# Two siblings' edits in one 24,000-instruction block kernel: opening loads, router zeroing and first gather, score banks, out-projection banks

## The reference, cut to what matters

```python
def first_block(x, ...):
    h = _layer_norm(x, ln_in_g, ln_in_b)
    mix = _token_mixer(h, ...)            # h @ w_in, gated delta rule over 8 heads, spatial gating, w_o
    h = _layer_norm(ALPHA * h + mix, ln1_g, ln1_b)
    ffn = _hier_moe(h, ...)               # top 2 of 32 experts for each token
    return _layer_norm(ALPHA * h + ffn, ln2_g, ln2_b)

def _hier_moe(x, ...):
    pg = softmax(x @ w_rg + b_rg); grp = argmax(pg)
    top_v, top_i = top_k((x @ w_re + b_re) of that group, 2)
    ...                                   # rows sorted by expert
    y = (silu(x_pad @ w1[e]) * (x_pad @ w3[e])) @ w2[e]

def second_block(x, meta_tokens, ...):
    h = concat(meta, x)                   # 16 + 512 rows
    q, k, v, xr, gr, g_merge = split(rmsnorm(h) @ w_in)
    attn = gqa(rope(rmsnorm(q)), rope(rmsnorm(k)), v)        # 8 heads, softmax(q k) v
    rnn = rg_lru(conv(xr), ..., lam) * gelu(gr)              # uses 8 * log_sigmoid(lam)
    h = h + (sigmoid(g_a) * attn + sigmoid(g_r) * rnn) @ w_out
    return (h + (silu(g) * u) @ w_ffn_out)[16:]              # g, u of rmsnorm(h) @ w_ffn_in
```

## Time and profile before

| | us |
|---|---|
| median of 3 runs | 2288.48 (2287.21 to 2293.3) |
| the profiled execution, its own time | 2291.81 |
| span in its profile | 2290.0 |
| TensorE busy | 2064.2 (90%) |
| VectorE, ScalarE, GpSimd busy | 950.8, 644.4, 454.5 |
| mean granted TensorE clock | 0.946 of full speed |

### The profile page before, as it was taken

The page is one execution under the profiler, slowest core; times in us unless marked ns, Lnnn a source line. Parts: engine busy times, 40 slices in busy tenths (PEclk is TensorE's granted clock), DMA queues, the critical chain, the costliest instruction groups (busy, mean ns, idle before and its releaser), DMA issues.

```text
span 2290.0 us, 24322 instructions
## 1 busy us (share of the span) xinstructions
PE 2064.2 (90%) x10160; PEld 1515.5 (66%) x10160; DVE 950.8 (42%) x1370; ACT 644.4 (28%) x969; POOL 454.5 (20%) x311
## 2 busy tenths in 40 slices
PE   5999999999999969888788879898898888999999
PEld 4879888888887753333333337676665666888787
DVE  6864444433323661111011125864554883222333
ACT  3442332321323201000000024343135754222221
POOL 4432132232332511111111011320002310000021
PEclk8899999999999979999899989999999998999999
DMA  4662231221324367999999964302111033322220
GB/s 156 202 184 61 56 88 42 38 74 38 74 37 150 138 246 306 407 410 410 403 412 412 417 280 173 108 2 82 46 47 46 37 111 110 110 94 90 84 82 37
DMA packets 97513, 360.75 MB, mean 158 GB/s; under 512 B 9834, under 2 KB 34572, under 8 KB 85112
## 3 DMA queue, kind: packets, MB, share of 16 engines
q1 hardware_dynamic: 84752, 332.76, 40.4%
q0 software_dynamic: 8240, 19.00, 2.5%
q10 hardware_dynamic: 4408, 7.40, 1.0%
HBM read 338.41 MB, written 29.10 MB: 160 GB/s over the span
## 4 chain that ended last, share of the span: by engine, by line
PE 79%; DVE 9%; ACT 5%; issue 5%; POOL 1%; DMA 1%; ACTq 0%; SPq 0%; DVEq 0%; POOLq 0%
PE ps L269 75%; PE ps L273 4%; ACT ST L265 1%; DVE H L259 1%; ACT L265 1%; DVE ST L253 1%; DVE BG L253 1%; ACT M L265 1%; DVE WL L253 0%; POOL WL L253 0%; DVE ST L2829 0%; DMA BG<-h1d,toki 0%; DVE BG L259 0%; DVE ML L253 0%; ACT M L266 0%
## 5 line engine op out<-in xcount | busy, mean ns | idle before, releaser
L269 PE MATMUL ps<-W,BG 128*64 128x512 f32 x672 | 202.1, 643 | 31.5 <-issue 31.4
L269 PE MATMUL ps<-XH,WS 128*128 128x512 f32 x704 | 218.6, 392 | 0.0
L269 PE MATMUL ps<-HTH,WL 128*128 128x512 f32 x448 | 182.4, 407 | 0.0
L269 PEld LDWEIGHTS ps<-ST 128*128 128x128 f32 x1376 | 168.4, 193 | 8.7 <-POOL ST L253 1.7
L269 PE MATMUL ps<-ST 128*128 128x64 f32 (+1 forms) x1376 | 168.7, 274 | 1.2 <-POOL ST L253 1.0
L269 PEld LDWEIGHTS ps<-XH,WS 128*128 128x128 f32 x704 | 133.5, 190 | 28.0
L269 PE MATMUL ps<-M,BG 128*64 128x512 f32 (+1 forms) x336 | 122.1, 550 | 31.2 <-DVE H L259 13.7
L2100 DVE COPY BG<-ps 128x512 f32<-128x512 f32 x32 | 22.1, 692 | 302.0 <-PE ps L269 302.0
L269 PE MATMUL ps<-XL,WS 128*128 128x512 f32 x352 | 138.3, 393 | 5.0 <-DVE XL L253 5.0
L269 PEld LDWEIGHTS ps<-W,BG 128*64 128x64 f32 x672 | 61.6, 147 | 120.8 <-issue 119.5
L263 ACT ACTIVATE BG<-ps 128x512 f32<-128x512 f32 x48 | 28.5, 595 | 381.3 <-PE ps L273 350.0
(11 more groups left out here) (384 smaller groups left out, 4392.9 us busy)
## 6 DMA issues: line engine op xcount, KB each, us to landing
W<-in_w SPq DMA_DIRECT2D x42, 2048.0 KB, 26.6
W<-in_w_in SPq DMA_DIRECT2D x27, 2048.0 KB, 10.4
ST<-in_w SPq DMA_DIRECT2D x14, 2048.0 KB, 25.6
U<-in_w SPq DMA_DIRECT2D x14, 2048.0 KB, 27.2
M<-in_w SPq DMA_DIRECT2D x13, 2048.0 KB
HT<-in_w SPq DMA_DIRECT2D x13, 2048.0 KB, 27.6
W<-in_w_ffn_in SPq DMA_DIRECT2D x22, 1024.0 KB, 7.7
ypad<-BG SPq DMA_DIRECT2D x23, 512.0 KB, 15.0
```

Source lines behind the costliest of these rows:

```text
L269: return p.e.matmul(o, lhsT=l, rhs=r, start=start, stop=stop, skip_group_check=True)
```

## The change

It joins edits of two siblings.
- *Opening.* The loads that ScalarE issued (small projection's weights and rows, layer norm rows, level masks) move to SyncE's list, behind the first weight load; the level masks come last, behind the second weight load. Jobs T0 and T1 are split ahead of d0, and d1 is split after T5. GpSimd subtracts d0's low part first and converts the level masks only in step 4 of `g_qk`; the meaning of counts 1 and 2 of `first_done` is exchanged accordingly.
- *Router and experts.* The zeroing of the gathered rows' buffers moves from GpSimd to ScalarE (a copy times zero). `s_expert_x(0)` stands ahead of the four loads for later stages, and the load of slot 6 (the seventh weights) also waits for the first gather.
- *Recurrence constants.* `v_lambda` and `s_lambda` move from the head of the middle stage into step 4 of the expert loop.
- *Attention.* `f.wide` holds the bank pair of the last `x` tile. Scores skip that pair if another is free, and if it is the next in the list, the transposes of the step before come first.
- *Out-projection.* Tile (m, y) lies in bank 2m + 1 - y; the steps of the norm behind it are reordered, and `s_turn3` is cut in halves.

The diff, with context lines and repeated renumberings of semaphore counts left out:

```diff
@@ -464,12 +464,19 @@
                     q.e.dma_start(cst[:, :], cst_d[:, 0:C_LV]).then_inc(c_cst, 16)
-            for n in range(2):
-                q_weight(n)
+            q_weight(0)
+            q.e.dma_start(wab_raw, w_in[:, 6144:6272].rearrange("(k p) n -> p k n", p=P)).then_inc(c_ab, 16)
+            q.e.dma_start(abr[:, 0:16], b_in[6144:6160].partition_broadcast(P)).then_inc(c_ab, 16)
+            q.e.dma_start(abr[:, 16:24], a["dn_dt_bias"][0].partition_broadcast(P)).then_inc(c_ab, 16)
+            q.e.dma_start(abr[:, 24:32], a["dn_a_log"][0].partition_broadcast(P)).then_inc(c_ab, 16)
+            for r, x in enumerate((a["ln_in_g"], a["ln_in_b"])):
+                q.e.dma_start(rows_in0[:, r, :], x.partition_broadcast(P)).then_inc(c_row[r], 16)
+            q_weight(1)
+            q.e.dma_start(lvf, cst_d[:, C_LV:C_N]).then_inc(c_lv, 16)
...
-            q.wait_ge(first_done, 2)
+            q.wait_ge(first_done, 1)
             for b in range(part, NZ, 3):
@@ -495,11 +502,6 @@
                 s_ln(0, i)
-            for r, x in enumerate((a["ln_in_g"], a["ln_in_b"])):
-                s.e.dma_start(rows_in0[:, r, :], x.partition_broadcast(P)).then_inc(c_row[r], 16)
-            s.e.dma_start(lvf, cst_d[:, C_LV:C_N]).then_inc(c_lv, 16)
-            s_ab_load()
-            s_split_w(0)
             s.wait_ge(*B["pc"].free())
@@ -508,16 +510,15 @@
                 s_split(("T", k))
-            s_split_w(1)
+                if k in (1, 5):
+                    s_split_w(k // 4)
...
             g.e.memset(z_t, 0.0).then_inc(g.up())
-            g.wait_ge(c_lv, 16)
-            g.e.tensor_copy(lv[:, :], lvf).then_inc(first_done)
+            low_split_w(g, 0)
             g.wait_ge(*g.now)
             g.e.memset(xpz, 0.0).then_inc(first_done)
-            low_split_w(g, 0)
             low_split_w(g, 1)
@@ -571,7 +572,7 @@
-        JOBS = [("d", 0)] + [("T", k) for k in range(8)] + [("d", 1), ("d", 2), "ab"] + [("d", n) for n in range(3, 24)]
+        JOBS = [("T", 0), ("T", 1), ("d", 0)] + [("T", k) for k in range(2, 6)] + [("d", 1), ("T", 6), ("T", 7), ("d", 2), "ab"] + [("d", n) for n in range(3, 24)]
         JOBS += [("v", 0, i) for i in range(4)] + [("v", 1, i) for i in range(4)]
@@ -684,7 +685,7 @@
             if n < 3:
-                s.wait_ge(first_done, 2)
+                s.wait_ge(first_done, 1)
             else:
@@ -936,6 +931,9 @@
                     low_split(g, "ab")
+                if n == 4:
+                    g.wait_ge(c_lv, 16)
+                    g.e.tensor_copy(lv[:, :], lvf).then_inc(first_done)
                 if n in (1, 3, 5, 7):
@@ -1753,6 +1751,8 @@
         def s_router():
...
+            act(BG[0:BLK, 8:16, :], cst[0:BLK, 0:512].unsqueeze(1).to_broadcast([BLK, 8, 512]), ACT.Copy, scale=0.0).then_inc(rt_out)
             s.wait_ge(rt_in, 1)
@@ -1762,7 +1762,6 @@
                 g.e.dma_start(h1d[m * P:(m + 1) * P, :], H[:, m, :]).then_inc(c_h1, 16)
-            g.e.memset(BG[0:BLK, 8:16, :], 0.0).then_inc(g.up())
@@ -2053,12 +2052,11 @@
         def s_experts():
-            s.wait_ge(*B["lg", 3].full())
+            s_expert_x(0)
             s_row(0, a["ln2_g"][0])
...
             s.e.dma_start(ST[:, 16:18, :].rearrange("p a b -> p (a b)"), rope_d).then_inc(c_rp, 16)
-            s_expert_x(0)
             for b in range(NE):
@@ -2067,6 +2065,8 @@
                         act(dg[n], ident, ACT.Copy, scale=gt[:, n // 2, n % 2:n % 2 + 1]).then_inc(dg_done)
+                if b == 4:
+                    s_lambda()
                 if b == NE - 2:
@@ -2100,6 +2100,8 @@
                     v_over_rows()
+                if b == 4:
+                    v_lambda()
                 if b == NE - 2:
@@ -2123,7 +2125,7 @@
             g.wait_ge(yrow_done, 1)
-            g.wait_ge(*g.now)
+            g.wait_ge(rt_out, 1)
             for b in range(NR):
@@ -2639,6 +2642,7 @@
                     pairs.append(b)
+                    f.wide = b
                     gr_read[j] = t.full()
@@ -2862,11 +2866,12 @@
             kv, j = h // 4, h % 2
...
             def scores(i):
-                b = pairs.pop(0)
+                b = pairs.pop(1 if pairs[0] == f.wide and len(pairs) > 1 else 0)
                 t = B.tile(("sc", h, i), b, wide=True)
@@ -2891,7 +2896,7 @@
                     yield
-                first = i < NT and bool(pairs)
+                first = i < NT and bool(pairs) and pairs[0] != f.wide
                 x = scores(i) if first else None
@@ -3149,7 +3154,6 @@
             ts(v, qg, pcol(QNG), 128.0 ** -0.5, None, MUL, None).then_inc(qg_done)
-            v_lambda()
             back = v_second(f)
@@ -3160,7 +3164,6 @@
             f = Front()
-            s_lambda()
             back = s_second(f)
@@ -3189,7 +3192,7 @@
-            out2 = [[B.tile(("out", m, y), 2 * m + y) for y in range(2)] for m in range(NT)]
+            out2 = [[B.tile(("out", m, y), 2 * m + 1 - y) for y in range(2)] for m in range(NT)]
@@ -3246,11 +3249,11 @@
             v_gain3(0)
+            v_rms3(2)
             v_added(3)
-            v_rms3(2)
-            v_low3(0)
             v_gain3(1)
             v_rms3(3)
+            v_low3(0)
             v_low3(1)
@@ -3269,7 +3272,7 @@
             z = slice(i * P, (i + 1) * P)
-            v.wait_ge(x3_hi, 2 * i + 2)
+            v.wait_ge(x3_hi, (3, 4, 6, 8)[i])
             tt(v, XL[:, :, z], HT[:, 0:8, z], XH[:, :, z].bitcast(F32), SUB).then_inc(x3_lo)
@@ -3288,23 +3291,26 @@
             s_normed3(1)
-            s_turn3(0)
+            s_turn3(0, 0)
+            s_normed3(2)
             s_squared(3)
-            s_normed3(2)
+            s_turn3(1, 0)
             s_normed3(3)
-            s_turn3(1)
-            s_turn3(2)
-            s_turn3(3)
+            s_turn3(0, 1)
+            s_turn3(1, 1)
+            for i in (2, 3):
+                for h in range(2):
+                    s_turn3(i, h)
...
-        def s_turn3(i):
-            s.wait_ge(*B["out", NT - 1, 1].full())
-            for h in range(2):
-                s.wait_ge(*B["x3", i, h].free())
-                act(x3_at(XH, i, h), x3_at(HT, i, h), ACT.Copy).then_inc(x3_hi)
+        def s_turn3(i, h):
...
+            s.wait_ge(*B["out", NT - 1 if h else 0, 1 if h else 0].full())
+            s.wait_ge(*B["x3", i, h].free())
+            act(x3_at(XH, i, h), x3_at(HT, i, h), ACT.Copy).then_inc(x3_hi)
@@ -3534,7 +3540,7 @@
                 w_room[N_EXP + EXP_SLOTS.index(i)] = [B["wo", NT - 1, 0].full(), B["wo", NT - 1, 1].full()]
-            w_room[N_EXP + EXP_SLOTS.index(6)] = [B["lg", i].full() for i in range(NT)]
+            w_room[N_EXP + EXP_SLOTS.index(6)] = [B["lg", i].full() for i in range(NT)] + [(c_xg[0], 16)]
             w_room[N_SEC + 1] = [(c_cb[i], CB0 + 32) for i in range(NT)]
```

More of the change, by code:

```diff
@@ L820, in build @@
         tmp_g = [x.rearrange("p (i n) -> p i n", i=4) for x in sp_tmp(128, 32)]
-        def s_ab_load():
-            s.e.dma_start(wab_raw, w_in[:, 6144:6272].rearrange("(k p) n -> p k n", p=P)).then_inc(c_ab, 16)
-            s.e.dma_start(abr[:, 0:16], b_in[6144:6160].partition_broadcast(P)).then_inc(c_ab, 16)
-            s.e.dma_start(abr[:, 16:24], a["dn_dt_bias"][0].partition_broadcast(P)).then_inc(c_ab, 16)
-            s.e.dma_start(abr[:, 24:32], a["dn_a_log"][0].partition_broadcast(P)).then_inc(c_ab, 16)
         def s_prep1():
@@ L1111, in v_head @@
             v.wait_ge(silu_done, qk_of(h))
-            v.wait_ge(first_done, 1)
+            v.wait_ge(first_done, 2)
             tt(v, Y, k4, four(t.at), MUL).then_inc(t.drained)
@@ L1242, in g_head @@
                 if n == 1:
-                    g.wait_ge(first_done, 1)
+                    g.wait_ge(first_done, 2)
                     g.wait_ge(xt0_done, h + 1)
@@ L1695, in build @@
         c_h1 = sem("h1_stored")
-        rt_in, rt_out, ms_done, dst_done = sem("router_in"), sem("router_exp"), sem("counts"), sem("rows")
+        rt_in, rt_out, ms_done, dst_done = sem("router_in"), sem("router_zero_and_exp"), sem("counts"), sem("rows")
         yrow_done = sem("y_rows")
@@ L1868, in v_rows @@
             ts(v, thr[1], io32[:, 1:8], float(BLK), -0.5, MUL, ADD).then_inc(v.up())
-            v.wait_ge(rt_out, 1)
+            v.wait_ge(rt_out, 2)
             v.e.tensor_reduce(pgs, gx, AX.X, ADD).then_inc(v.up())
-            v.wait_ge(rt_out, 2)
+            v.wait_ge(rt_out, 3)
             ts(v, den, ex, 1.0, None, ADD, None).then_inc(v.up())
@@ L2487, in __init__ @@
                 self.due = []
+                self.wide = None
         GRAN = [("v", 0), ("k", 0), ("k", 1)] + [("q", n) for n in range(8)] + [("a", n) for n in range(8)] + \
```

## The result

| | before | changed |
|---|---|---|
| median (runs) | 2290.89 us (4) | 2264.22 us (4) |
| lowest to highest | 2287.21 to 2296.97 | 2261.36 to 2271.41 |
| the profiled execution, its own time | 2291.81 | 2264.13 |
| its span | 2290.0 | 2262.3 |

A forecast was written before the change was run, and what follows sets the result against it. It took TensorE (busy 2064.2 of 2290.0 us) as the bound, and the weight stream in the expert stage. Six gains summed to 37.5 us, taken from a median of 2288.48: 2251.0 us, range 2243 to 2262.

The forecast's parts named there:

- Attention, the failed step: Last pair of heads: `f.wide` is never reset, so two bank pairs instead of three, a loss of 1.5 to 2.0 us.
- the sign itself: Attention: the prediction is wrong if the list of pairs leaves scores waiting for their own probabilities; no size given.
- Attention, the x stage: x tiles: waits on the convolution go, about 1.1 us each remains; 11.5 us gained before the last heads' loss.
- Opening: Kernel start: d1 starts at 31.2 instead of 41.05 us, gain 9.9 us.
- the upper bound: Opening: gain 11.5 us if the 1.6 us that the lower clock costs after a pause are saved.
- Router: Before the first gather: without zeroing, VectorE's cast ends sooner, then waits for the fourth logit tile; gain 2.5 us.
- First gather: Before expert 0: queues cleared of loads, the gather takes 4.0 us to landing instead of 9.13; gain 5.1 us.
- The rival that the loads do not matter: First gather stays long since DMA engines take turns between queues; 5.1 us less gain, 2256 us; chance 0.12.
- Held-back loads: Experts: 3.7 MB held back until the gather, costed at nothing; up to 9 us if the cover is gone.
- Recurrence constants: Head of the middle: a 1.28 us table load leaves ScalarE ahead of a 1.33 us wait; gain 1.3 us.
- Out-projection: Tile (0,0) moves from bank 0 to bank 1: 7.1 us of wait, 1.7 of restart, 0.4 of norm order; gain 9.2 us.
- The rival of the two pairs: Attention: scores avoiding `f.wide` wait for one another; gain 0 to 2 instead of 9.5 us, 2260 us; chance 0.10.

The follow-up runs named there:

- `reset`: Changed kernel plus one line that forgets the last x tile's bank pair (`f.wide = None`) after the x granules; 2248.27 us, 0.9824 of the kernel before.
- `scores_first`: Changed kernel where scores still avoid the last x tile's pair but are never put behind the transposes; 2260.11 us in one run.
- `pair_rule_alone`: Kernel before with the attention's edit alone; 2296.71 us, ratio 1.0016.
- `zero_on_gpsimd`: Changed kernel with the router's zeroing back on GpSimd; 2268.93 us in one run.
- `no_pair_rule`: Changed kernel with the attention's edit undone, so scores take the first pair and come first; 2265.33 us, ratio 0.9892.
- `opening_alone`: Kernel before with the opening's edits alone; 2281.96 us, ratio 0.9961.

## Why the prediction was wrong, step by step

- **Attention, the failed step.** It was the sentence that the last pair of heads "works on two pairs instead of three, three steps of 0.3 to 0.5, together 1.5 to 2.0". It measures 17.5 in the first profile (13.5 to 17.8 in the seven profiles of the changed kernel and of its variants with this loop), 15.5 more than said, and the forecast with this number in place is 2266.5, 2 us from the measured median. I had seen that `f.wide` outlives the x stage, and priced the missing pair. What I did not price is the other line: while the remembered pair is first in the list, `first` is false, so transposes come first, and each waits for a softmax that has just begun (9.1 us of waits in all profiles); and in this loop of waits TensorE falls to the lower clock, for 4 to 9 us more. `reset` takes all of it away with one line, `scores_first` shows that it hangs on this line. The prediction named the sign itself, "if the list of pairs leaves scores waiting for their own probabilities", though here it is the transposes that wait.
- **Attention, the x stage:** 11.5 of gain said before the loss, 12.0 measured; the residual wait 1.1 said, 1.36 measured. Right for the waits on the convolution. That the total agrees so well is partly luck: a wait of 2.9 us for probabilities was not foreseen, the waits fell by 9.6 us in all, and the clock gave the rest (in `pair_rule_alone` the same 9.6 us of waits gave 8.4).
- **Opening:** d1's start was right (31.2 said, 30.4 measured); the size was off, 9.9 said and 10.8 to 14.0 measured. What was missing is the clock. In the first profile of before TensorE runs at the lower level behind the pause ahead of d1 (granted clock 0.57 from 41 to 45 us; the upper bound had it, 11.5), which the changed kernel does not have, and neither has the second profile of before, behind the same pause (1.00 from 40 to 44 us). The rest is a later stretch at the lower level, near 80 us before (0.57 from 78 to 86 us, and from 75 to 83 in the second profile), which is shorter in the changed kernel (0.79 from 68 to 76 us) but not in most of its variants. So about 10 us are the change's, the rest the clock's.
- **Router:** 2.5 said, 2.5 measured, and shown by `zero_on_gpsimd`.
- **First gather:** 5.1 said, 6.0 measured; 4.0 us to landing said, 3.09 measured. Right, though the store it was measured by was the better of two: the other one of 512 KB, issued at 834.30 beside a 2 MB load, landed in 10.6 us, and that row already spoke for the loads. The rival that the loads do not matter because the engines take turns fell: with the 2 MB load beside it the gather takes 7.2, alone 3.1. The Trainium skill, "DMA: Bandwidth & Descriptors", section "Queues, rings and completion order", says that the engines take turns between queue rows; that may hold here (7.2 is a little over twice 3.1), but it was wrong to conclude from it that a neighbour costs nothing.
- **Held-back loads:** said to cost nothing, nothing seen within the experts' own spread of 5 us. No more than that is shown.
- **Recurrence constants:** 1.3 said, 2.1 to 2.9 measured ahead of the x stage; the wait is the 1.3, the rest is clock. That the same move changes the clock 150 us later was nowhere in the forecast; it seems to cost nothing here because the waits that it struck in `no_pair_rule` are gone.
- **Out-projection:** 9.2 said, 9.2 measured (7.0 and 2.2), though its smallest part, 0.4 for the norm's order, is nothing and the restart is larger than the 1.7 said; that the two cancel is luck.
- **Slips that moved nothing:** the lower bounds of the terms add up to 17, not 22 (7 + 0 + 0 + 0 + 4 + 6), and the expert stage is 502 us long, not 452.

The rival of the two pairs was there, at 0.10, with an attention gain of "0 to 2". Even it was too mild: the attention as a whole lost 5.5 us against the kernel before, 2.2 by the second profiles.

## What to carry to other kernels

A rule that holds only while a buffer is draining must be taken back when it has drained; look for the last place where the remembered value is read, and walk through the program's end with it. A change of order that fills a wait in one loop can serialise another that shares the code: price every loop that reaches the line, at the depth of work that it then has ahead. And a wait has two prices, its length and the clock at which TensorE restarts; after small shifts elsewhere the same wait of 3.3 us was followed by four matmuls in 1.16 or in 2.13 us. So the waits that a change removes do not give its gain by themselves: the same 9.6 us of waits in the x stage were worth 12.0 us in one kernel and 8.4 in another.

## What the runs showed of the hardware that I had not expected

- The clock behind a wait can change with an edit long before it: with the constants moved away, and with them one wait of 1.33 us some 150 us ahead, three of the later waits are followed by the lower level in both profiles (X + H 190.9 and 191.0), and with it back they are not (184.67, the same as two profiles of the kernel before). All waits are equal in these profiles. It is no rule for the single wait: `opening_alone`, with the constants in their old place, has one of the three followed by the lower level, and the kernel before has it at the other two waits of the x stage (1649.10 and 1666.36 us, four matmuls in 2.13). The windows around the first of them, first without, then with it:

```profile
1564.00:1574.00 10.00, 9.20 (x46) 7.82 (x47) 3.12 (x5) 2.15 (x5) 0.00 (x0) 0.70 0.25 81
```

```profile
1568.00:1578.00 10.00, 8.43 (x59) 7.60 (x60) 5.61 (x10) 3.00 (x7) 0.00 (x0) 1.00 0.31 94
```

- VectorE and GpSimd subtracting at the same time: one of the two is drawn out, and with the same starts, GpSimd 0.02 us ahead, it was VectorE in one profile (0.7 us became 2.89, at a cost of 3.7 us up to the first recurrence step) and GpSimd in others (2.36 became 2.95).
- A gather of 64 rows of 4 KB takes 2.9 to 3.1 us with next to nothing beside it in the queues, 7.2 beside one 2 MB load, and 7.5 to 9.1 beside that and four smaller loads.
